# Moving the normalisation sums of a two-block transformer kernel into the stage ahead, and reordering around them

## The reference

```python
def rmsnorm(x, g):
    xf = x.astype(jnp.float32)
    y = xf * lax.rsqrt(jnp.mean(xf * xf, axis=-1, keepdims=True) + EPS)
    return (y * g.astype(jnp.float32)).astype(x.dtype)

def modulate(x, g, shift, scale):
    return rmsnorm(x, g) * (1 + scale) + shift

def layer_norm(x, g, b):
    xf = x.astype(jnp.float32)
    mu = xf.mean(-1, keepdims=True)
    var = jnp.mean(jnp.square(xf - mu), -1, keepdims=True)
    return ((xf - mu) * lax.rsqrt(var + LN_EPS)).astype(x.dtype) * g + b

        h = h + g1 * y
        h = h + g2 * swiglu(modulate(h, norm2_g[l], sh2, sc2), ffn_w_in[l], ffn_w_out[l])
```

## Time and profile before

| | us |
|---|---|
| median of 3 runs | 4306.95 (4301.94 to 4308.75) |
| the profiled execution | 4309.97 |
| its span in the trace | 4308.2 |
| TensorE busy, matmuls | 3921.8 (91%) |
| VectorE, ScalarE, GpSimd busy | 1400.5, 1211.6, 1265.6 |
| mean granted TensorE clock | 0.913 |

### The profile page before, as it was taken

One profiled execution on the slowest core, in us unless ns is written; L12 is line 12 of the kernel. 1 busy time (PEld: TensorE's weight loads), 2 busy tenths in 40 slices (PEclk: granted clock), 3 DMA queues, 4 the chain that ended last, 5 costly groups with the idle time before them and its releaser, 6 DMA issues. The chain is left out here.

```text
span 4308.2 us, 77765 instructions
## 1 busy us (share of the span) xinstructions
PE 3921.8 (91%) x32782; PEld 3283.0 (76%) x32782; DVE 1400.5 (33%) x2756; ACT 1211.6 (28%) x2098; POOL 1265.6 (29%) x669
## 2 busy tenths in 40 slices
PE   6797899999889899979799999889999989998997
PEld 4685788888777677758688888778888868766886
DVE  1327311111345211165455655432111140444112
ACT  0216211111236222222233333322111132443222
POOL 0210222222325333323133222222222222553442
PEclk7899899999899899979777777789999989998998
DMA  8110132232200344323110000113323211112222
GB/s 291 54 50 9 66 117 105 90 117 83 69 18 21 127 151 157 131 81 115 70 37 24 24 24 26 41 59 117 105 90 117 83 54 59 36 35 79 97 83 73
DMA packets 119166, 343.31 MB, mean 80 GB/s; under 512 B 34031, under 2 KB 40559, under 8 KB 118511
## 3 DMA queue, kind: packets, MB, share of 16 engines
q1 hardware_dynamic: 118895, 339.40, 23.0%
HBM read 324.55 MB, written 16.93 MB: 79 GB/s over the span
## 5 line engine op out<-in xcount | busy, mean ns | idle before, releaser
L204 POOL TENSOR_TENSOR feed_low<-ring,feed_high 128x1024 fp32r<-128x1024 f32 (+1 forms) x240 | 627.0, 2614 | 1367.9 <-ACT feed_high L197 1367.9
L221 PE MATMUL ps<-hn_high,feed_high 128*128 128x512 f32 (+1 forms) x2112 | 759.8, 360 | 28.4 <-DVE hn_low L781 12.3
L221 PE MATMUL ps<-hn_low,feed_high 128*128 128x512 f32 (+1 forms) x2112 | 753.2, 357 | 0.0
L221 PE MATMUL ps<-hn_high,feed_low 128*128 128x512 f32 (+1 forms) x2112 | 751.8, 356 | 0.0
L221 PEld LDWEIGHTS ps<-hn_high,feed_high 128*128 128x128 f32 x2112 | 402.7, 191 | 113.5 <-issue 35.9
L221 PEld LDWEIGHTS ps<-hn_high,feed_low 128*128 128x128 f32 x2112 | 402.0, 190 | 57.4
L221 PEld LDWEIGHTS ps<-hn_low,feed_high 128*128 128x128 f32 x2112 | 402.7, 191 | 55.2
L197 ACT ACTIVATE feed_high<-ring 128x1024 fp32r<-128x1024 f32 (+1 forms) x240 | 273.0, 1139 | 481.2 <-PE ps L221 481.2
L1211 DVE TENSOR_TENSOR ps<-feed_gate,ps 128x768 f32<-128x768 f32 (+1 forms) x88 | 73.0, 829 | 1015.0 <-PE ps L221 991.9
L221 PE MATMUL ps<-feed_hid_high,feed_high 128*128 128x512 f32 (+1 forms) x1056 | 375.9, 356 | 5.3 <-DVE feed_hid_low L1214 5.3
L221 PE MATMUL ps<-feed_hid_low,feed_high 128*128 128x512 f32 (+1 forms) x1056 | 375.0, 355 | 0.0
(11 more groups left out here) (534 smaller groups left out, 7460.3 us busy)
## 6 DMA issues: line engine op xcount, KB each, us to landing
feed_side_ring<-in_ada SPq DMA_DIRECT2D x144, 512.0 KB, 5.8
ring<-in_ffn_g SPq DMA_DIRECT2D x88, 512.0 KB, 3.7
ring<-in_ffn_u SPq DMA_DIRECT2D x88, 512.0 KB, 3.7
ring<-in_ffn_d SPq DMA_DIRECT2D x64, 704.0 KB, 4.1
ring<-in_ada SPq DMA_DIRECT2D x48, 512.0 KB, 5.2
ring<-in_od_in SPq DMA_DIRECT2D x24, 512.0 KB, 3.7
ring<-in_ev_in SPq DMA_DIRECT2D x23, 512.0 KB, 4.5
ring<-in_even_in SPq DMA_DIRECT2D x20, 512.0 KB, 4.2
```

The lines of the kernel that those rows point to most:

```text
L204: pool.tensor_tensor(self.low[:, j % self.slots, 0:w], feed.ring[:, slot, 0:w], self.high[:, j % self.slots, 0:w].bitcast(F32), ALU.subtra ...
L221: mm = pe.matmul(dst, weights[a], values[b], start=first and n == 0, stop=last and n == 2)
```

## The change

The sums of every norm but the first are made in the stage ahead: `StreamSums` squares each chunk of `h` on ScalarE as soon as its residual is added, and TensorE sums it behind the next tile; ahead of a layer norm TensorE sums `h` itself. Only the squares of a layer norm, which need the mean, stay. The sums of the first norm and its whole root go into `modulation`, interleaved with the groups of the modulation's products, and the gating stage is `rooted`: it starts with the scaling. Because the sums take a PSUM bank, `project_out` turns over three PSUM regions, no longer four. GpSimd waits with the weights' low parts until the root is split (`after_split`), writes two of them ahead of the norm's chunks, not four, and in the gating stage it alternates. In `early_products` the second tile is two chunks behind the first, and each tile is reported on its own. `sm.products.vector` stands behind the norm. The first tile of `feed_down` waits for the last chunk of its input only where it uses it. In the lora stage the two pooled tiles come first, and the pooling ahead of the mixing; GpSimd's clearing stands behind its norm chunks.

```diff
+LORA_ORDER = (3, 4, 0, 1, 2)
-        ("lora", 1, [(j % 4, rw, 0, 18 + j) for j in range(5)]),
+        ("lora", 1, [(n % 4, rw, 0, 18 + j) for n, j in enumerate(LORA_ORDER)]),
 # modulation
+        norm = rms_stream(k, st, TOK, "mixer", 0, bank=5, r=3)
+        sums = StreamSums(k, st, TOK, 5, loaded, 0, [norm.sq[:, c, :] for c in range(4)])
+            act.sem_inc(loaded, KC)
+            for c in range(KC):
+                sums.scalar(act, c)
+            norm.scalar(act)
+                if g < KC:
+                    sums.tensor(pe, g)
+                elif g == KC + 1:
+                    norm.tensor(pe)
+                if g == KC:
+                    norm.sums.build(dve)
+                    dve.wait_ge(sums.summed, KC)
+                    norm.factor(dve)
+def quarter_sums(k, pe, bank, values, q, first, last):
+    for i in range(4):
+        mm = pe.matmul(k.ps[32 * i:32 * i + 32, bank, 0:q], k.ones[:, 0:32], values[:, q * i:q * (i + 1)], start=first, stop=last)
+    return mm
+class StreamSums:
+    def scalar(self, act, c):
+        act.wait_ge(self.updated, self.base + c + 1)
+        if c >= len(self.sq):
+            act.wait_ge(self.summed, c - len(self.sq) + 1)
+        act.activation(self.sq[c % len(self.sq)], self.k.h[:, c, 0:self.tokens], ACT.Square).then_inc(self.squared, 1)
+    def tensor(self, pe, c):
+        if self.sq:
+            pe.wait_ge(self.squared, c + 1)
+            values = self.sq[c % len(self.sq)]
+        else:
+            pe.wait_ge(self.updated, self.base + c + 1)
+            values = self.k.h[:, c, 0:self.tokens]
+        quarter_sums(self.k, pe, self.bank, values, self.tokens // 4, c == 0, c == KC - 1).then_inc(self.summed, 1)
 # NormedStream
+    def after_split(self, pool):
+        pool.wait_ge(self.split_ready, 1)
     def vector(self, dve):
+        if not self.rooted:
+            self.sums.build(dve)
+            if self.offset is not None:
+                self.centre(dve)
+            else:
+                self.factor(dve)
+        self.prepare(dve)
+        if self.offset is not None:
+            dve.wait_ge(self.summed, KC)
+            self.factor(dve)
+        self.apply(dve)
+    def apply(self, dve):
+        dve.drain()
 ...
-        dve.wait_ge(self.spread, 1)
+        if not self.rooted:
+            dve.wait_ge(self.spread, 1)
 def early_products(k, pe, norm, split, tiles):
-    slots = [split.wait(pe, 0, e) for e, *_ in tiles]
-    for c in range(KC):
-        cols = slice(c * P, (c + 1) * P)
-        norm.wait(pe, c)
+    LAG = 2
+    for step in range(KC + LAG * (len(tiles) - 1)):
+        if step < KC:
+            norm.wait(pe, step)
+        for n, (e, dst, tokens) in enumerate(tiles):
+            c = step - LAG * n
 ...
+            if c == KC - 1:
+                mm.then_inc(split.products, 1)
 # project_out
-            for n in range(2, KC):
-                split.write_high(act, n // 4, n % 4)
+            for n in range(KC):
+                if n + 2 < KC:
+                    split.write_high(act, (n + 2) // 4, (n + 2) % 4)
+                if squares:
+                    sums.scalar(act, n)
-                if n >= 4:
-                    pe.wait_ge(free, n - 3)
-                tile_products(k, pe, i, j, region(k, j, tokens), mixed, tokens, split)
+                if n >= 3:
+                    pe.wait_ge(updated, n - 2)
+                tile_products(k, pe, i, j, region(k, n % 3, tokens), mixed, tokens, split)
+                sums.tensor(pe, n - 1)
+            sums.tensor(pe, KC - 1)
 # feed_forward
+        sums = StreamSums(k, st, tokens, 4, y_free, 10, [gate] if squares else None)
+                        if e == 0:
+                            norm.after_split(pool)
                         for j in range(2):
                             split.write_low(pool, 0, j, e)
-                pe.wait_ge(hid_low_ready, HALF * (h + 1))
+                pe.wait_ge(hid_low_ready, HALF * (h + 1) - 1)
 ...
+                for c in range(HALF):
+                    if c == HALF - 1:
+                        pe.wait_ge(hid_low_ready, HALF * (h + 1))
 ...
+                for n in range(1, DOWN):
+                    pe.wait_ge(y_free, 8 * h + n + 1)
+                    tile_products(k, pe, n // 4, n % 4, region(k, n % 2, tokens), hid, tokens, split, chunks=range(HALF))
+                    if h:
+                        sums.tensor(pe, n - 1)
+                if h:
+                    sums.tensor(pe, DOWN - 1)
-                for n in range(1, DOWN):
-                    split.write_high(act, n // 4, n % 4, e2)
+                for n in range(DOWN):
+                    if n + 1 < DOWN:
+                        split.write_high(act, (n + 1) // 4, (n + 1) % 4, e2)
+                    if h and squares:
+                        sums.scalar(act, n)
-            if next_c:
-                sm.products.vector(dve)
                 if h == 0:
                     norm.vector(dve)
+                    if next_c:
+                        sm.products.vector(dve)
 # project_in, GpSimd (ScalarE's high parts alike)
             if norm:
-                for e in range(RING):
+                norm.after_split(pool)
+                for e in range(2):
                     split.write_low(pool, 0, e)
                 norm.gpsimd(pool)
-            for e in range(RING if norm else 1, at):
+            for e in range(2 if norm else 1, at):
 # gating_mlp
-        norm = rms_stream(k, st, TOK, "mixer", 0, r=1, squares=k.mo[:, 0:4, :])
+        norm = rms_stream(k, st, TOK, "mixer", 0, rooted=True, r=3, squares=k.mo[:, 0:4, :])
-            for e in range(4):
+            for e in range(2):
                 split.write_low(pool, 0, e)
-            norm.gpsimd(pool)
-            for e in range(4, 8):
+            for e, c in zip((2, 3, 4), norm.by_pool):
+                norm.gpsimd(pool, c)
+                split.write_low(pool, 0, e)
+            for e in range(5, 8):
                 split.write_low(pool, 0, e)
-            norm.tensor(pe)
+            early_products(k, pe, norm, split, [(ENTRY[0], region(k, U_REGION[0]), TOK)])
             for e in range(1, 5):
                 split.wait(pe, 0, e)
-            early_products(k, pe, norm, split, [(ENTRY[0], region(k, U_REGION[0]), TOK)])
 # lora_and_pooling
+            norm.after_split(pool)
             split.write_low(pool, 0, 0)
             split.write_low(pool, 0, 1)
-            pool.memset(raw[:, :, :], 0.0)
-            pool.memset(pads[0][:, :, :], 0.0).then_inc(zeroed, 1)
             norm.gpsimd(pool)
+            pool.memset(pads[0][:, :, :], 0.0)
+            pool.memset(raw[:, :, :], 0.0).then_inc(zeroed, 1)
             pe.wait_ge(pooled_ready, 1)
-            pe.wait_ge(copied, 4)
+            pe.wait_ge(copied, 3)
-            for j, dst in enumerate((wd, ad, gd)):
-                dve.wait_ge(copied, j + 1)
-                shift_mix(dve, dst, raw[:, j, :], own[:, j:j + 1], mu(0, j), mu(1, j)).then_inc(mixed, 1)
-            dve.wait_ge(copied, 5)
+            dve.wait_ge(copied, 2)
 ...
             ins.then_inc(pooled_ready, 1)
+            for j, dst in enumerate((wd, ad, gd)):
+                dve.wait_ge(copied, j + 3)
+                shift_mix(dve, dst, raw[:, j, :], own[:, j:j + 1], mu(0, j), mu(1, j)).then_inc(mixed, 1)
```

More of the change, by code:

```diff
@@ L638, in add @@
     def add(self, pe, bank, values, first, last):
[L639 to L642 removed]
+        return quarter_sums(self.k, pe, bank, values, self.q, first, last)
     def total(self, bank):
@@ L746, in roots, with high @@
         act.activation(self.sums.factor[:, :], self.sums.factor[:, :], ACT.Sqrt).then_inc(self.root_ready, 1)
-    def high(self, act):
+    def high(self, act, chunks=range(KC)):
         k = self.k
-        for c in range(KC):
+        for c in chunks:
             act.wait_ge(self.scaled, c + 1)
@@ L873, in early_products @@
 def early_products(k, pe, norm, split, tiles):
-    slots = [split.wait(pe, 0, e) for e, *_ in tiles]
-    for c in range(KC):
-        cols = slice(c * P, (c + 1) * P)
-        norm.wait(pe, c)
-        for slot, (_, dst, tokens) in zip(slots, tiles):
+    LAG = 2
[4 more added lines that the diff above has]
+            c = step - LAG * n
+            if not 0 <= c < KC:
+                continue
+            slot, cols = split.wait(pe, 0, e) if c == 0 else e % split.slots, slice(c * P, (c + 1) * P)
             for a, b, _ in spans(tokens):
@@ L882, in early_products, with layer_norm @@
                                        (k.hn[0][:, c, a:b], k.hn[1][:, c, a:b]), c == 0, c == KC - 1)
-    mm.then_inc(split.products, len(tiles))
-def layer_norm(k, tokens, which):
+            if c == KC - 1:
+                mm.then_inc(split.products, 1)
+def layer_norm(k, tokens, which, bank):
     with ExitStack() as k.tmp, Stage(k, "layernorm") as st:
@@ L902, in _ @@
         def _(pe):
-            for c in range(KC):
-                mm = sums.add(pe, 0, k.h[:, c, 0:tokens], c == 0, c == KC - 1)
```

(17 more changed lines are left out.)

167 lines of the change are left out of this document (83 added, 84 removed).

## The result

The changed kernel takes 4267.99 us (median of 10 runs, 4253.70 to 4296.96) where the kernel before takes 4304.44 (10 runs, 4299.28 to 4321.74): a ratio of 0.9913, 95% interval 0.9889 to 0.9937, some 37 us less. The forecast was 67.5 us less, 4240 in a range of 4220 to 4265. The sign was right, the time lies 3 us outside the range.

A forecast was written before the change was run, and what follows sets the result against it. TensorE, busy 91%, was held by its standstills, at gating's start nearly all one VectorE chain with GpSimd inside; 17 + 28.0 + 14.1 + 0.5 − 16.8 + 11.3 + 8.1 + 5.3 = 67.5 us less, 4240, range 4220 to 4265.

The forecast's parts named there:

- the woven sums' term: Two output projections and two channel mixers of each kind: sums between tiles cost TensorE 16.8 us, nothing for changing product kind.
- First norm: Moved into the modulation, it lets gating's token products start earlier: 18 gained less 1 for the modulation, 17 us, bounds 13 to 23.
- RMS starts: First and second channel mixer, window and lora: shorter sums, freed splits and an earlier pick gain 28.0 us, bounds 24 to 32.
- Layer-norm starts: Third and fourth mixer and neighbour stage: freed splits and sums of h gone ahead of the mean gain 14.1 us, bounds 12 to 16.
- The last norm: The kernel's last norm, predicted to gain 0.5 us.
- The lag: Early tiles: the second tile behind the first shortens TensorE's waits for low weights and copies, gaining 11.3 us, bounds −3 to 16.
- the lag backfires: Rival, chance 0.12: thin early products keep TensorE at the lower clock longer, losing 14 us, giving 4254.
- Lora: Lora from its first product on: 9.5 us gained, 1.4 from the lag and 8.1 at its end.
- The end: Lora's end: pooling runs beside three tiles, so the mixing is late next; 8.1 us gained, bounds 6 to 10.
- Last chunk: feed_down in the fourth mixer: two gaps of 2.63 us go, gaining 5.3 us; nothing changes in the other three mixers.
- GpSimd in the way: Rival, chance 0.22: prepare and first low parts are caught at every RMS and rooted start; 15 us less gain, 4255.
- ScalarE starves the ring: Rival, chance 0.03: in the channel mixers squares delay the queued high weights, and TensorE waits; over 4315 us.

The follow-up runs named there:

- pool_early: The changed kernel without GpSimd's wait for the root's split, so its first low weights follow the high weights again; 4272.73 us, ratio 0.9916.
- one pair: Both kernels with one of six head pairs in the rwkv stage, the other chunks zeroed; 3784.8 us before, 3759.12 us changed.
- again: The changed kernel run once more, unaltered, for a second trace; median 4287.4 us (8 runs), ratio 0.9924 to the kernel before.
- best: The changed kernel without lag, sums behind last tiles ahead of layer norms, some squares summed in groups, lora's memsets first and fifth tile's weights issued early; 4231.25 us.
- lora_free: The changed kernel with lora's memsets ahead of its low parts and the fifth tile's weights issued before the kept stream's copy; 4260.98 us, ratio 0.9878.

## Why the prediction missed

**The step that failed is the woven sums' term.** "I find no row for a cost of changing between the two kinds of product; were it 0.1 each, it would be 22." It is 0.37 and 0.33 each; the sums themselves (0.305 and 0.253) were priced about right from the earlier trace rows. The term was 16.8 and measured 29.5: 12.7 of the 25.5 us between 67.5 and 42.0. Split by these prices, with six sums a stage and not the seven of the forecast, the sums themselves make 13.4 us and the changes, which stood in the sum at nothing, 16.8. A row of eight sums in one run holds one change for sixty-four products, so it could not show this; the bound should have reached for it, and with 29.5 the forecast would have been 4252.

**First norm: right.** 15.3 of 17. The modulation grew by about 2.5 us, not 1.

**RMS starts: right, and stage by stage.** 28.7 of 28.0: 9.2 in the first mixer (its terms make 9.7), 7.3 in the window stage (7.3), 7.6 in the second mixer (7.3) and 4.6 in lora (3.7). At 768 tokens the small operations were not caught, and lora's kept scale was, as forecast (2.34 us against 2.4).

**Layer-norm starts: 12.6 of 14.1.** The split gave its 3.7. But the spread of the mean now follows a standstill: in the third mixer VectorE waits 2.54 us for it, where it waited 1.79 while the eight sums of `h` ran just ahead; in the neighbour stage it is 2.54 and 1.45, in the fourth mixer 2.06 and 1.20. In all three the clock during the spread is 0.50 in the changed kernel's first trace, and in the kernel before 0.75, 1.00 and 1.00. Together that is 2.7 us; other terms came out better. The last norm has the same (clock 0.50 and 1.00, wait 2.06 and 1.20 us), which is most of why it lost 0.5 instead of gaining it.

**The lag: the waits went, the gain did not come.** TensorE's waits for the mixers' low weights fell from 11.1 us to 2.6 (4.0 in the second trace; without the lag 7.7), with one of 2.0 left in the fourth mixer. Yet six stages gave 3.2 of 9.9, and with the lag taken out they took the same time. The rival "the lag backfires" named a reason, the lower clock under thin early products; the second mixer shows it, 2.3 us longer with the lag, while for the other five stages it is not shown. In lora the lag is worth 2.4.

**Lora: the wrong cover.** The end came as forecast and somewhat better, 9.5 of 8.1: the pooling's product stands straight behind the last tile (1898.41), and ScalarE's copy ends 12 us behind that tile, not 21. (The terms of the forecast add up to 13.2 us, not 13.4.) From its first to its last tile lora lost 2.5 us, where the forecast had 1.4 gained. What I had not queued are the two memsets, which the change moves behind the low parts, and the fifth tile's weights: in the kernel before these landed 51.6 us behind the last residual and ScalarE took them at 51.9, when the tile ahead was done, so they were in time only because TensorE had stood still for 3.66 us. That stall went, and TensorE waits 3.40 us for the fifth tile instead.

**Last chunk: right**, 5.6 of 5.3. **GpSimd in the way** did happen as a mechanism, in lora alone, and `pool_early` shows what it would have cost at every start. It is the first of the rivals; the paragraph on the RMS starts calls it the second. **ScalarE starves the ring** did not: from first to last residual the mixers with squares take as long as those without (85.40 us both at 768 tokens, 56.63 both at 512).

What stays open: 37 us by the medians, 42 by three traces each, and 26 to 33 with one pair. The pairs' stage, the third mixer, the first mixer and lora differ by 31, 8, 6 and 4 us between executions of one kernel. Which form an execution falls into, and whether the change shifts the odds, was not settled.

## What to carry to other kernels

Count the changes between kinds of product, not only the products: a short sum between large tiles cost 0.67 us at 768 tokens, twice what it costs in a row (0.31 to 0.35), so collect sums and place them where TensorE waits anyway. Queue GpSimd's work where VectorE has none of its small or plain operations: a run of GpSimd work without a pause can be charged as a whole to the first such operation that meets it, and whether it is differs between executions. When a wait is removed, look at which DMA was in time only because of it.

## What the runs showed of the hardware

One stage of unchanged instructions takes 31 us more or less with the granted TensorE clock (means 0.74 and 0.80), while the busy times of VectorE, ScalarE and GpSimd stay within 3.2 us of each other. Its shortest form repeats: 491.25, 491.26, 491.24 and 491.22 us in four traces of four kernels (`again`, `pool_early`, `best`, `lora_free`). A comparison of under 1% is better made on the lengths of the parts than on medians of a few runs.

A change between the 128*128 products and the 128*32 sums costs TensorE 0.37 us at 768 tokens and 0.33 at 512, there and back, with no idle time in the profile.

GpSimd holds some operations of VectorE and not others. TENSOR_SCALAR on 256 columns took 0.35 us alone, 1.4 to 2.0 beside one low part, and beside three operations in a row 5.30 and 5.28 in two traces and 1.96 in a third. SCALAR_TENSOR_TENSOR on 512 columns with one input in PSUM stayed at 0.75 beside GpSimd's weights; whether the kind of operation or the input in PSUM makes the difference, no run separates.
